# Attention's last step, the phase border and the way into the experts: loads, splits and the last norm factor moved

## The reference, cut to what matters

```
u = RMSNorm(h);  proj = u @ w_in
o_mla  = attention(8 heads, causal, 128-query blocks)      # branch A
o_hg   = gated linear recurrence                           # branch B
merged = gate_m * (o_mla @ w_br_mla) + gate_h * (o_hg @ w_br_hgrn)
h = h + merged @ w_out
u = RMSNorm(h, ffn_norm)
g_logits = u @ w_group + b_group;  e_logits = u @ w_route + b_route
# best of 8 groups, then the best two of its 8 experts, weights from softmax
y[token] += weight * (silu(u @ w1[e]) * (u @ w3[e])) @ w2[e]     # 64 experts, width 256
out = RMSNorm(h + y)
```

## Time and profile before

| | us |
|---|---|
| median of 3 runs (1502.99 to 1505.22) | 1503.21 |
| the profiled execution, whole time | 1504.32 |
| its span | 1502.5 |

### The profile page before, as it was taken

The page is one execution under the profiler, slowest core; times in us unless marked ns, Lnnn a source line. Parts: engine busy times, 40 slices in busy tenths (PEclk is TensorE's granted clock), DMA queues, the critical chain, the costliest instruction groups (busy, mean ns, idle before and its releaser), DMA issues. The chain is left out here.

```text
span 1502.5 us, 21051 instructions
## 1 busy us (share of the span) xinstructions
PE 1383.1 (92%) x8471; PEld 986.7 (66%) x8471; DVE 581.4 (39%) x1302; ACT 559.9 (37%) x1065; POOL 102.1 (7%) x131
## 2 busy tenths in 40 slices
PE   6999999999999999999979999899987787788877
PEld 5888887787888887766658888755543444344443
DVE  6455565432531054567657555311101011101117
ACT  6534354222332156444542355333322222222223
POOL 0000000000000000000000011211111111111100
PEclk9999999999999999999999999999999999989999
DMA  6111111112224333112136645899999999999998
GB/s 184 43 29 43 29 34 38 32 30 84 84 85 134 87 95 138 36 36 71 64 105 236 261 172 177 319 362 416 415 417 416 416 416 416 416 416 417 416 393 345
DMA packets 130592, 312.52 MB, mean 208 GB/s; under 512 B 31280, under 2 KB 77360, under 8 KB 113344
## 3 DMA queue, kind: packets, MB, share of 16 engines
q1 hardware_dynamic: 118464, 285.96, 50.9%
q0 software_dynamic: 12032, 25.22, 4.4%
HBM read 283.81 MB, written 41.98 MB: 217 GB/s over the span
## 5 line engine op out<-in xcount | busy, mean ns | idle before, releaser
L2355 PE MATMUL ps<-r,m_xT 128*64 128x256 f32 x2048 | 259.1, 410 | 65.3 <-DMA r<-in_w 64.0
L130 PE MATMUL ps<-uTh,h_wh 128*128 128x512 f32 (+3 forms) x696 | 263.8, 379 | 4.4 <-DVE uTl L566 2.4
L131 PE MATMUL ps<-uTl,h_wh 128*128 128x512 f32 (+3 forms) x696 | 256.0, 368 | 0.0
L132 PE MATMUL ps<-uTh,h_wl 128*128 128x512 f32 (+3 forms) x696 | 255.6, 367 | 0.0
L2355 PEld LDWEIGHTS ps<-r,m_xT 128*64 128x64 f32 x2048 | 153.5, 147 | 153.5 <-DMA r<-in_w 71.8
L2275 DVE TENSOR_TENSOR m_prod<-m_sig,ps 128x128 f32<-128x128 f32 x64 | 18.4, 288 | 338.8 <-ACT m_sig L2246 338.8
L130 PEld LDWEIGHTS ps<-uTh,h_wh 128*128 128x128 f32 (+1 forms) x696 | 129.4, 186 | 28.7 <-DVE uTl L566 4.3
L132 PEld LDWEIGHTS ps<-uTh,h_wl 128*128 128x128 f32 (+1 forms) x696 | 129.5, 186 | 20.1
L131 PEld LDWEIGHTS ps<-uTl,h_wh 128*128 128x128 f32 (+1 forms) x696 | 129.6, 186 | 19.5 <-issue 0.2
L2339 PE MATMUL ps<-r,m_hT 128*64 128x512 f32 x512 | 122.4, 598 | 1.3 <-DVE m_hT L2279 0.9
L2236 ACT ACTIVATE m_y<-ps,gate 64x512 f32<-64x512 f32 x128 | 87.3, 682 | 80.0 <-PE ps L2339 78.5
(11 more groups left out here) (360 smaller groups left out, 2097.7 us busy)
## 6 DMA issues: line engine op xcount, KB each, us to landing
r<-in_w SPq DMA_DIRECT2D x190, 1024.0 KB, 24.0
h_w<-in_w_in SPq DMA_DIRECT2D x37, 512.0 KB, 4.3
gates<-h_sg POOLq DMA_DIRECT2D x16, 512.0 KB, 2.9
r<-y_moe SPq DMA_DIRECT2D x8, 1024.0 KB, 16.9
br_gate<-gates SPq DMA_DIRECT2D x14, 512.0 KB, 4.2
e_wo<-in_w_out SPq DMA_DIRECT2D x4, 1024.0 KB, 6.4
f_x<-in_x SPq DMA_DIRECT2D x8, 512.0 KB, 5.1
h_mid<-f_x SPq DMA_DIRECT2D x8, 512.0 KB, 3.9
```

What stands on the lines that cost most here:

```text
L130: pe.matmul(out, lh, rh, start=start, stop=False)
L131: pe.matmul(out, lh, rl, start=False, stop=False)
L132: return pe.matmul(out, ll, rh, start=False, stop=stop)
L2355: ins = pe.matmul(bank(UP_BANK + e % 2, 0, DE, CAP * f, CAP * (f + 1)).rearrange("p (r f) -> p r f", r=2), xT[i % 2][:, j, CAP * k:CAP * ( ...
```

## The change

In the attention:
- the split of weight 8 moves from step 29 to step 31, ahead of that of weight 9, on ScalarE and on VectorE;
- in step 30 VectorE takes the second head's maximum (`peak(31, 1)`) before it normalizes the first head (`normed(31, 0)`);
- the loads of weights 10 and 11 move across the barrier, into the merge's SP list behind `load_out(0)`; the merge's `high(2)` and `high(3)` on ScalarE now wait for them;
- the 12 loads into `M` become 2 of 1.5 MB each, and nothing but the last fill and the last stored gate holds them.

Between output and experts:
- for the last tile alone u = h * gain is made by halves (`gained`), and ScalarE multiplies it with the factor, in place; VectorE makes only the reciprocal (`last_factor`) before it goes on to `choose`;
- POOL's first gather waits for one zeroed buffer, its own; the second gather for ScalarE's first;
- SP waits until the first gather has landed before it loads expert 6's weights;
- the first turn signals after 4 of its 8 blocks, ScalarE copies that half at once, and expert 0's products begin with it.

```diff
@@ attention, sync
             sp.wait_ge(ro_mm, 1)
...
-            sp.wait_ge(wl_ok, DK + 1)
-            load_w(DK + 2)
             sp.wait_ge(f_mm, 2 * DK)
             for b in range(2):
                 sp.wait_ge(stored[b], 16 * (DK // 2 - 1))
-            for n in range(2, DK):
-                for q in range(2):
-                    sp.dma_start(g.M[q][:, n, :], g.gates[D + n * P:D + (n + 1) * P, q * 512:(q + 1) * 512]).then_inc(m_in, 16)
-            sp.wait_ge(wl_ok, DK + 2)
-            load_w(DK + 3)
+            for q in range(2):
+                sp.dma_start(g.M[q][:, 2:DK, :], g.gates[D + 2 * P:2 * D, q * 512:(q + 1) * 512].rearrange("(n p) t -> p n t", p=P)
+                             ).then_inc(m_in, 16)
...
-                sp.wait_ge(w_in[b], 16 * (DK // 2 + 2))
+                sp.wait_ge(w_in[b], 16 * (DK // 2 + 1))
@@ attention, scalar (vector alike with split)
-                if i % 4 == 1 and k >= 5:
+                if i % 4 == 1 and 5 <= k < len(steps) - 3:
                     split_high(act, (k + 3) // 4)
                 elif k == len(steps) - 1:
+                    split_high(act, DK)
                     split_high(act, DK + 1)
@@ attention, vector
-                if more:
+                if k + 2 == len(steps):
+                    peak(k + 1, 1)
+                    normed(k + 1, 0)
+                    normed(k + 1, 1)
+                elif more:
@@ merge
         load_out(0)
+        load_w(2)
+        load_w(3)
         load_out(1)
...
-            if n >= 4:
-                act.wait_ge(w_in[n % 2], 16 * (n // 2 - 1))
+            act.wait_ge(w_in[n % 2], 16 * (n // 2))
@@ output, sync
             store_h(TT - 1)
+            sp.wait_ge(g.x_in[0], 16)
             g.load_up(sp, 6, 6)
             g.load_down(sp, 6, 6)
@@ output, gpsimd
-            pool.wait_ge(z_ok, XB)
+            pool.wait_ge(z_ok, 1)
...
             for i in range(XB - 1):
+                wait(pool, zs_ok, i)
@@ output, scalar
                 table(t, ACT.Exp, 1)
+                if t == TT - 1:
+                    act.wait_ge(hg_ok, 2)
+                    act.wait_ge(r_ok, 1)
+                    act.activation(u[:, :], u[:, :], ACT.Copy, scale=sc[:, 14:15]).then_inc(u_ok, 1)
                 shares(t)
@@ output, vector
+            def gained(q):
+                cols = slice(q * 512, (q + 1) * 512)
+                dve.wait_ge(u_out, 16 * (TT - 1))
+                dve.wait_ge(h_ok, 2 * (TT - 1) + q + 1)
+                dve.tensor_tensor(u[:, cols], x[(TT - 1) % 2][:, cols], gain[:, cols], ALU.mult).then_inc(hg_ok, 1)
+
+            def last_factor():
+                dve.wait_ge(rt_ok, TT)
+                c.link(dve.reciprocal(sc[:, 14:15], st[:, 3:4]))
+                dve.sem_inc(r_ok, 1)
...
-                scaled(t)
+                if t < TT - 1:
+                    scaled(t)
+                else:
+                    last_factor()
@@ experts, scalar
                 for q in range(2):
+                    if i == 0 and q == 0:
+                        act.wait_ge(x_half, 1)
+                    elif i == 0:
+                        act.wait_ge(x_tr, 1)
@@ experts, tensor
+                    if i == 0 and j == DK // 2 - 1:
+                        ins.then_inc(x_half, 1)
...
-                    pe.wait_ge(xT_ok, 2 * i + 2)
+                    pe.wait_ge(xT_ok, 2 * i + (1 if e == 0 else 2))
                     for j in range(DK):
+                        if e == 0 and j == DK // 2:
+                            pe.wait_ge(xT_ok, 2)
```

More of the change, by code:

```diff
@@ L1310, in vector @@
                     gated_if_done(half)
-                if i % 4 == 1 and k >= 5:
+                if i % 4 == 1 and 5 <= k < len(steps) - 3:
                     split((k + 3) // 4)
                 elif k == len(steps) - 1:
+                    split(DK)
                     split(DK + 1)
@@ L1502, in load_w @@
         def load_w(n):
-            sp.wait_ge(wl_ok, n - 3)
+            if n >= 4:
+                sp.wait_ge(wl_ok, n - 3)
             sp.dma_start(w[n % 2][:, :, :], w_src[:, :, n * P:(n + 1) * P]).then_inc(w_in[n % 2], 16)
@@ L1735, in gpsimd @@
             record(TT - 1)
+            pool.wait_ge(zs_ok, XB - 1)
         def scalar(act):
@@ L1807, in scalar @@
             act.wait_ge(u_ok, TT)
-            act.activation(xr[1], g.ones[:, 0:1].to_broadcast([P, D]), ACT.Copy, scale=0.0).then_inc(z_ok, 1)
+            act.activation(xr[1], g.ones[:, 0:1].to_broadcast([P, D]), ACT.Copy, scale=0.0).then_inc(zs_ok, 1)
             act.wait_ge(lg_mm, TT)
-            act.activation(xr[2], g.ones[:, 0:1].to_broadcast([P, D]), ACT.Copy, scale=0.0).then_inc(z_ok, 1)
+            act.activation(xr[2], g.ones[:, 0:1].to_broadcast([P, D]), ACT.Copy, scale=0.0).then_inc(zs_ok, 1)
         def vector(dve):
@@ L1919, in vector @@
                     first_sum(t)
+                    gained(1)
                     dve.wait_ge(h_tr, 2 * TT)
@@ L2220, in copied @@
             def copied(i):
-                act.wait_ge(x_tr, i + 1)
+                if i:
+                    act.wait_ge(x_tr, i + 1)
                 if i >= 2:
```

5 lines of the change are left out of this document (4 added, 1 removed).

## The result

| | us |
|---|---|
| before, median of 4 runs (1501.85 to 1505.22) | 1503.1 |
| after, median of 4 runs (1494.1 to 1496.1) | 1494.49 |
| ratio, with its 95% interval | 0.9941 (0.9929 to 0.9954) |
| profiled execution after, whole time and span | 1496.1, 1494.4 |

What follows compares the result with a forecast made beforehand. The prediction took the landing of expert weights, a DMA stream at 416 GB/s, as the bound. Border 4.3 plus way to expert 0 5.0 gave 9.3 us off the median 1503.21, so 1494, range 1489.5 to 1498.5.

Steps and rivals of the forecast that it cites:

- part A: Border from attention to merge: barrier opens 4.0 us sooner, clock adds 0.3; 4.3 us in all, bounds 2.5 to 6.
- part B: Last tile to expert 0: of 7.7 us DMA time lost, 2.4 stay and 0.3 is left; gain 5.0, bounds 2.5 to 6.5.
- Rival 3: At the border: the barrier isn't set by SP's load, only the gain towards expert 0 comes; 1498.2 us, chance 0.07.
- The clock at the merge: TensorE's clock behind the shorter border idle time: between 0 and 2.0 us more gain, taken as 0.3.
- rival 1: At the merge: TensorE starts at full clock, 1.7 us more gain, 1492.2 us; chance 0.20.
- The lists: Ahead of the experts: `ranks` 0.7 to 0.8 us sooner, lists' rows 0.9 sooner, the first gather issued 1.2 sooner.
- The gather: First gather ahead of expert 0: 5.3 us from start to landing, at 964.8, with expert 6's load held back.
- The gap: DMA engines before expert 6's first bytes: idle 965 to 967.4, 2.4 us lost in place of 7.7.
- rival 2: First gather stays slow whatever SP holds back, landing near 967.1; 4.7 us lost, not 2.4; 1496.2 us, chance 0.17.
- What B is not: Experts: expert 0 starts 6 to 8 us earlier, but bytes decide, so halves and faster clock are not added.
- Rival 4: Start of experts: late first gather leaves DMA idle with 3.15 MB deferred; 0.2% slower if landing at 977.4; chance 0.02.

Runs made afterwards that it cites:

- loads_back: Changed kernel with only the loads of weights 10 and 11 put back ahead of the barrier, each behind the split that frees its buffer; 1499.4 us, ratio .9962.
- border_only: Kernel before with only the attention and merge part of the change, all between output and experts undone; 1498.2 us, ratio .9953.
- changed_again: The changed kernel run once more, unaltered, as the yardstick for further runs; 1493.4 us, ratio .9928 to the kernel before.
- no_halves: Changed kernel with the first turn of gathered rows in one piece, copy and products only after all 8 blocks; 1494.1 us, ratio .9927.
- factor_on_dve: Changed kernel with the last tile's factor back on VectorE, one 1024-column operation between reciprocal and logits; 1492.7 us, ratio .9922.
- no_hold: Changed kernel, but SP loads expert 6 without waiting for the first gather; 1497.2 us, ratio .9953 to the kernel before.
- hold_on_lists: Changed kernel, but expert 6's load waits for the rows' lists and not for the first gather's landing; 1496.6 us, ratio .9944.
- timed_hold: Changed kernel, but the 25th of 32 matmuls in the second keep_up releases expert 6's load, not the gather's landing; 1495.1 us, ratio .9938.
- down_first: Changed kernel with SP's load of expert 4's w2 ahead of the store of the last u; 1493.9 us, ratio .9931.
- step_back: Changed kernel with the attention's last step in the old order (weight 8's split, second head's maximum), loads left as changed; 1497.4 us, ratio .9954.
- way_only: Kernel before with only the part of the change between output and experts; 1499.0 us, ratio .9965.

## Why the prediction came out right, point by point

**The sum.** Forecast 4.3 + 5.0 = 9.3 against the profiled execution. Measured between the two profiles: 8.1, of which the attention ahead of all changed loads gave back 1.8, so 9.9 for the changed stretches: 4.6 for part A (4.1 + 0.5), 5.3 for part B (6.3 - 1.0). Both lie 0.3 above the forecast. That they lie so near is partly luck: in B a cost at the end of 1.0 and a gain of 1.2, neither forecast nor explained in full, nearly cancel, and in A the profiled execution had a slow clock at the merge that the nine other profiles with this border did not have.

**Part A, the border: right, and shown.** SP's last landing set it (loads_back 15.24, changed 11.65), the new order shortens the engines' own end by 1.49 (last weighing 10.69 to 9.2), and a border with either edit undone stays at 15.2 to 15.3. The gates' loads no longer matter. TensorE ran on through the merge without waiting for weight 2. Rival 3 is refuted by border_only. The sum has a slip: 1.5 sooner, less 0.1 for the split, is 1.4 and not 1.6, so it should have said 3.8 and not 4.0. Measured from the last scores, VectorE now ends 3.9 us ahead of the old landing, and the merge follows in 1.6 in place of 1.8: that makes the 4.1. What I had not seen is that behind the old order's 2.6 us gap the clock can fall, so that undoing the order cost 3.7 and not 1.5.

**The clock at the merge: the chance was wrong.** I took 0.3, with 1.7 more as rival 1 at 0.20. The profile of after shows about 0.5 (13th matmul at 4.3 in place of 4.8). But nine other profiles with the same border, idle 2.45 too, all start the merge at full speed, with the 13th matmul at 2.8: a gain of 1.9. So rival 1 is what happens in nine profiles of ten, and the first profile was the odd one. My reason against it, short gaps around the border, did not hold. That is worth 1.5 us more, and changed_again, no_halves and factor_on_dve (1492.7 to 1494.1, beside a before at 1504.5 to 1504.7) show a larger gain, 10.6 to 12.0, than the first runs' 8.6. How much of this is the clock, how much the chip and how much the scatter of the merge (158.1 to 159.6 us from merge to T at full clock) the runs don't separate.

**The lists: right.** Logits to the T of the run: 4.75 to 3.79, of 1.2 forecast 0.96, for the logits now start 0.16 behind the reciprocal; ranks 8.39 to 7.63, the 0.7 to 0.8 of the forecast, right behind keep_up; lists' rows 11.02 to 10.14 (0.9); gather issued 12.64 to 11.45 (1.2).

**The gather: the term was mis-sized.** "I take 5.3, landing at 964.8". It took 7.1, and in the six other profiles with the same hold and the same order of loads 6.1 to 7.2. The step that failed is the 5.1 us (8.9 - 3.8) that I ascribed to the queue ahead, of which I counted on 3.6 (8.9 - 5.3). Shown in its place: load queued ahead 8.65, load issued beside it 8.60, load held 6.1 to 7.2, expert 4's load earlier 3.9. The hold takes off 1.4 to 2.6. The Trainium skill (DMA: Bandwidth & Descriptors, section Queues, rings and completion order) says that each DMA engine takes turns between the queues with work. By that rule it would not matter where in its queue SP's load stands, and no_hold and hold_on_lists agree. The price of 1.3 that I worked out from that rule is itself too high, for the gather moves less than the 0.5 MB that I took. Transfers of before from 1080 to 1430 us, POOL's queue and its issues:

```profile
q0 software_dynamic: 6171, 11.42, 8.6%
y_moe<-m_y,dst POOLq DMA_INDIRECT x22, 8.0
rows<-u_moe,src POOLq DMA_INDIRECT x21, 9.6
```

That is 0.27 MB for each of 43 issues on average, 0.6 us at 416 GB/s. So the rule's price would be 0.6 and mine was 3.6, and the 1.4 to 2.6 lie between; what makes up the rest is open.

**The gap: right by two errors.** The rows landed 1.8 late, at the time that rival 2 had, nearly (T + 18.5; the rival 19.0, the forecast 16.7). But the gap did not cost the 4.7 of rival 2. I had it empty; in truth the indirect transfers and then expert 6's first bytes fill it with 40 to 188 GB/s, so that a gap of some 5 us loses 3.0, against 2.4 forecast. SP's queue ran dry at about T + 16.7, as forecast (965 - 948.12 = 16.9).

**What B is not: right behind the hold, with one sign missed.** The first product of expert 0 moved from T + 24.7 to 20.1, and varied from 19.4 to 24.7 over all kernels. The last product less the DMA time lost is 498.0 before and in border_only, and 496.5 to 497.7 in all twelve others. Expert 7's load is a rival measure: it moves with the last product too, over all kernels (the one less the other is 477.8 to 479.6). What tells them apart are three kernels beside changed_again: in no_halves expert 7's load comes 1.3 us later and the last product only 0.4, in timed_hold it comes at the same time and the last product 0.8 later, with 0.9 more DMA time lost, and in down_first it comes 0.5 later and the last product 0.4 earlier, with 0.8 less lost. Bytes decide. The sign that failed: the stretch from expert 0's first product to the last one was to be longer than before, and it is 484.4 us before and 482.7 after, because the end moved more than the start. Of the 6.3 us gained, 5.1 are DMA time no longer lost; the 1.2 in the constant I have not traced, nor could I have forecast them, as little as the 1.0 that the end gave back.

**Rival 4** never came near: the slowest first gather was 8.9.

## What to carry to other kernels

Before a barrier, look at what SP still has in flight for the block behind it: two loads of 256 KB that nobody needed yet cost 2.6 us with the old order of the last step and 3.6 with the new one, and moving them behind the barrier cost nothing. In a stage bound by bytes, count only the DMA time lost at its edges; a first product that started 1.3 us later cost 0.4 while a load filled the time, but where the next load waits for that product, its start does set the bytes; and a gather's bytes inside a gap count as work. Holding a bulk load back for a small indirect transfer pays if the transfer releases that stream, but price it from runs with and without the load beside it, not from what stands ahead in a queue.

## What the runs showed of the hardware that I had not expected

- Idle times of about 2.5 us were followed by either level of TensorE's clock, though it had been full ahead of each but one. Behind 2.45 us at the border it was full in nine profiles and half in one (in step_back, at 2.46, it had been half before and rose to full while TensorE stood idle); behind 2.59 to 2.60 ahead of the last turn full in one (before) and half in two (way_only, step_back). Behind 3.65, 5.09 and 6.04 it was half. In factor_on_dve it fell in a stretch whose longest idle time was 1.11.
- An indirect transfer of the same rows took 3.9 to 8.9 us from issue to landing by what moved beside it, and the scatter beside a 3 MB load held POOL 8.72 us in place of 3.15; 0.7 us between two issues of that load made 5.8 us of difference to the scatter (8.72 against 2.92).
- The last 45.3 or 46.2 us, split by where one operation 500 us earlier runs: the eleven longer ones all have one instruction packet on the DMA engines beside the last store, which then lands in 3.6 us in place of 2.6.
